# Expert stage of a diffusion step: prompt pieces in groups of three ahead of every third sample chunk

## The chip, the cores and the metric

The kernel runs on one NeuronCore of a Trainium2 chip, in one launch. The metric is the device time of the execution in microseconds (us), taken as the median of several runs. Besides the times there is one profiled execution, whose trace gives every instruction's start and length, what each engine waited for, and the clock that TensorE was granted.

## What is computed

The reference is one layer of a backbone with 1024 latent (sample) tokens and 256 context (prompt) tokens of width 1024, all in float32. After the first sub-layer (convolution and attention) comes the mixture of experts, which takes most of the time:

```python
def expert_choice_ffn(h, w_router, w_gate, w_up, w_down):
    cap = EC_CAPACITY * T // N_EXPERTS          # 128 of 1024 sample tokens, 32 of 256 prompt tokens
    aff = softmax(h @ w_router)
    g, idx = top_k(swapaxes(aff, 1, 2), cap)
    xe = h[idx]
    hid = silu(xe @ w_gate) * (xe @ w_up)       # 1024 -> 2048
    ye = (hid @ w_down) * g                     # 2048 -> 1024
    return zeros.at[idx].add(ye)
```

It is done for the sample tokens and for the prompt tokens with the same weights, for 16 experts. Each expert has 24 MB of weights.

## The kernel before, in words

**Chunks.** The weights of an expert come in 12 chunks of 2 MB (NCH), each with two DMAs from SP's queue into one of six slots: chunks 0 to 7 (NG8 of them) are 256 hidden columns of the gate and of the up matrix, chunks 8 to 11 (ND4) are four blocks of 128 rows of the down matrix. Slot c % 6 takes the next chunk as soon as the sample product of the chunk in it is done.

**Sample product** (`sample(e, c)`, line 1106). For accuracy each weight is split in two parts: ScalarE (ACT) rounds half a chunk at a time into e_hi (`weight_round`, lines 1596 and 1598), of which there are two buffers, and VectorE (DVE) writes the rest over the slot (`weight_rest`, lines 2165 and 2169). TensorE (PE) then runs 24 matmuls 128x512 over the full 128*128 array. The gated result goes ACT (silu, line 1618), DVE (product hid, line 2186), PE (`turn_hid`, two transposes), ACT and DVE (hT_hi and hT_lo, lines 1621 and 2190). Chunk n can be rounded only when sample chunk n-2 has left its e_hi buffer.

**Prompt product** (`prompt(e, c)`, line 1078). It reads the raw weights of the slot, so it must run before `weight_rest` of that chunk. Its 32 rows fill a 128*32 part of the array, four at a time: 128 MATMUL records of 128x128 for two gate and up chunks, 64 of 128x256 for two down chunks. For a gate and up chunk the piece that results goes: `prompt_copy` (ACT, line 1603, bank to pv), `turn_prompt` (PE, line 1146, one transpose), `prompt_gate` (ACT silu, line 1608), `prompt_hid` (DVE product, line 2175). Piece c is in bank 2 + c % 2 throughout, so from chunk 2 on `prompt(e, c)` waits for the product of piece c - 2 (semaphore hp_ok, line 1086).

**Order on PE** (`expert`, line 1151, written out by hand). Ahead of every even sample chunk c a block of two prompt chunks is run, c + 2 and c + 3 (past the end: those of the next expert); then the sample chunk, then `turn_hid(c - 1)`, then `turn_prompt(c + 2)`. After sample chunk 8 come the 16 transposes of the next expert's gathered tokens (`gathered_in`); DVE turns those of the prompt into xpT (`prompt_rows`, line 2145). ACT and DVE have matching orders of their own (lines 1613 and 2178): each of them is a queue in which a wait holds all that follows. Transposes are recorded at line 686, other matmuls at line 683.

Of the kernel before, what the change touches and what calls it, by code (L numbers as in the profile page):

```python
# [25 lines left out]
ALU = mybir.AluOpType  # L26
# [7 lines left out]
P = 128  # L34
# [49 lines left out]
def backbone(nc, A, O):  # L84
    ctx = ExitStack()
    with ctx:
# [110 lines left out]
        sil = at(M7 + 8704, 2, 256)  # L197
        pv = at(M7 + 9216, 2, P)
        psil = at(M7 + 9472, 2, 64)
        xg = at(M7 + 9600, 2, D)  # L200
# [480 lines left out]
        def _(pe):  # L681
# [396 lines left out]
            def prompt(e, c):  # L1078
# [3 lines left out]
                if c < NG8:  # L1082
                    if c == 0:
                        pe.wait_ge(xe_dve, e * KD + KD)
                    if c >= 2:
                        pe.wait_ge(hp_ok, e * NG8 + (c - 1))
                    for k in range(KD):
                        for g in range(4):
                            last = mm(bank[2 + c % 2][32 * g:32 * g + 32, 0:P], xpT[:, k, :],
                                      slot[q][:, 8 * (g // 2) + k, P * (g % 2):P * (g % 2) + P], k == 0, k == KD - 1)  # L1090
                else:
                    f0 = 4 * (c - NG8)
                    pe.wait_ge(hp_ok, e * NG8 + (f0 // 2 + 2))
                    for f in range(f0, f0 + 4):
                        for g in range(4):
                            last = mm(bank[7][32 * g:32 * g + 32, 0:256], hpT[:, f, :],
                                      wide(slot[q])[:, f - f0, 256 * g:256 * g + 256], f == 0, f == KE - 1)
# [44 lines left out]

            def turn_prompt(e, c):

                pe.wait_ge(pv_ok, e * NG8 + (c + 1))
                tr(bank[2 + c % 2][:, 256:256 + P], pv[:, c % 2, :], P).then_inc(pt_ready, 1)

# [3 lines left out]
            def expert(e, last_one):  # L1151

                for c in range(NCH):
                    if e == c == 0:
                        sample(e, c)
                    if c % 2 == 0:
                        for n in (c + 2, c + 3):
                            if n < NCH or not last_one:
                                prompt(*ahead(e, n))
                    if e or c:  # L1160
                        sample(e, c)
                    if 1 <= c <= NG8:
                        turn_hid(e, c - 1)
                    en, cn = ahead(e, c + 2)
                    if cn < NG8 and (en == e or not last_one):
                        turn_prompt(en, cn)
                    if c == NG8 and not last_one:
                        pe.wait_ge(hp_ok, e * NG8 + NG8)
                        gathered_in(e + 1)
# [5 lines left out]
            prompt(0, 1)  # L1175
            turn_prompt(0, 0)
            turn_prompt(0, 1)
            for e in range(NE - 1):
# [5 lines left out]
        def _(act):  # L1184
# [414 lines left out]

            def prompt_copy(e, c):  # L1600

                act.wait_ge(pr_ready, e * NCH + (c + 1))
                A_(pv[:, c % 2, :], bank[2 + c % 2][:, 0:P], ACT.Copy).then_inc(pv_ok, 1)

            def prompt_gate(e, c):

                act.wait_ge(pt_ready, e * NG8 + (c + 1))
                A_(psil[:, c % 2, :], bank[2 + c % 2][:, 256:320], ACT.Silu).then_inc(psil_ok, 1)

# [3 lines left out]
            def expert(e, last_one):  # L1613

                for c in range(NCH):
# [10 lines left out]
                    en, cn = ahead(e, c + 1)  # L1626
                    if cn < NG8 and (en == e or not last_one) and (e, c) != (0, 0):
                        prompt_gate(en, cn)
                    if en == e or not last_one:
                        weight_round(en, cn, 0)  # L1630
                    if c % 2 == 0:
                        for n in (c + 2, c + 3):
                            ep, cp = ahead(e, n)
                            if cp < NG8 and (ep == e or not last_one):
                                prompt_copy(ep, cp)
                    if en == e or not last_one:
# [12 lines left out]
            xe_leave(0, 0, KD)  # L1649
            xe_round(0)  # L1650
            prompt_copy(0, 0)
            prompt_copy(0, 1)
            prompt_gate(0, 0)
            prompt_gate(0, 1)
            for e in range(NE - 1):
# [14 lines left out]
        def _(dve):  # L1670
# [500 lines left out]

            def prompt_hid(e, c):

                dve.wait_ge(psil_ok, e * NG8 + (c + 1))
                V_.tensor_tensor(hpT[:, 2 * c:2 * c + 2, :], bank[2 + c % 2][:, 320:384].rearrange("p (a n) -> p a n", a=2),
                                 psil[:, c % 2, :].rearrange("p (a n) -> p a n", a=2), ALU.mult).then_inc(hp_ok, 1)

            def expert(e, last_one):
# [4 lines left out]
                for c in range(NCH):  # L2183
# [8 lines left out]
                    en, cn = (e, c + 1) if c + 1 < NCH else (e + 1, 0)  # L2192
                    if 0 < c and cn < NG8 and (en == e or not last_one):
                        prompt_hid(en, cn)
                    if c == NG8 + 1 and not last_one:
# [11 lines left out]
                    elif not last_one:  # L2207
                        weight_rest(e + 1, 0)
                if not last_one:
                    prompt_hid(e + 1, 1)  # L2210
                dve.wait_ge(down_ready, e * ND4 + 8)
# [10 lines left out]
            weight_rest(0, 0)  # L2222
            prompt_hid(0, 0)
            prompt_hid(0, 1)
            for e in range(NE - 1):
# [33 lines left out]
```

## Time and profile before

| what | value |
|---|---|
| median of 3 runs | 2732.86 us (2730.2 to 2734.89) |
| the profiled execution | 2732.86 us, of which its span is 2731.1 us |
| PE busy, share of the span | 2606.7 us, 95% |
| DVE, ACT, POOL busy | 65%, 48%, 9% |
| mean granted clock of TensorE | 0.981 of full speed |
| bytes moved | 543.82 MB, mean 199 GB/s; 281 GB/s in the expert stage |

The span runs from the first to the last instruction. A busy share is an average over the whole span. Times of rows count from the span's start. The expert stage begins at about 1171 us, with the first gathered tokens, and ends at about 2690 us. Matmuls overlap one another: a record's length is its latency, and the time that a matmul takes in a stream is the distance between the starts of two of them.

### The profile page before, as it was taken

Reading aid. Unit: us, or ns where it says so; the run is one execution under the profiler, and the core shown is the slowest. Engines: PE = TensorE matmul, PEld = TensorE weight load, DVE = VectorE, ACT = ScalarE, POOL = GpSimd, SP = SyncE. Lnnn points to the kernel's source line nnn. Section 1 sums busy time; section 2 is a strip of 40 time slices with the busy share of each in tenths; the row PEclk is TensorE's granted clock in tenths of the full one; section 3 lists DMA queues with packets and bytes.
Section 4 is the critical chain, followed back from the end, with each engine's and each line's share of the span. In section 5 each row is a group of like instructions: output and inputs, shape, how many; then the busy total and the mean of one; then the engine's idle time right before and its main releaser. Section 6 shows DMA issues by size and latency. Waiting matters only on the chain.

```text
span 2731.1 us, 50488 instructions
## 1 busy us (share of the span) xinstructions
PE 2606.7 (95%) x22107; PEld 2070.5 (76%) x22107; DVE 1776.8 (65%) x2129; ACT 1315.1 (48%) x1911; POOL 239.3 (9%) x194
## 2 busy tenths in 40 slices
PE   5999999999999999779999999999999999999994
PEld 4888866666878887567788778777877877787783
DVE  5699847776343354757667767767767767767664
ACT  5111145555232232456556556555555556556554
POOL 0122012210000000001011001101100110111000
PEclk9999999999999999889999999999999999999997
DMA  8431311001333651668889888879988987988884
GB/s 265 155 93 32 81 48 27 15 24 47 93 93 93 183 172 61 213 206 281 281 279 294 271 279 291 280 265 298 295 259 286 297 269 270 297 273 281 281 268 172
DMA packets 457509, 543.82 MB, mean 199 GB/s; under 512 B 26304, under 2 KB 409387, under 8 KB 457290
## 3 DMA queue, kind: packets, MB, share of 16 engines
q1 hardware_dynamic: 449610, 519.60, 58.3%
q0 software_dynamic: 7680, 20.98, 3.5%
q8 instruction: 176, 2.88, 0.5%
q14 instruction: 43, 0.35, 0.0%
HBM read 513.27 MB, written 27.28 MB: 198 GB/s over the span
## 4 chain that ended last, share of the span: by engine, by line
PE 90%; DVE 3%; ACT 2%; SPq 1%; issue 1%; DMA 1%; POOL 0%; DVEq 0%; POOLq 0%; ACTq 0%
PE bank L683 86%; PE bank L686 4%; SPq L404 1%; DVE arena L1889 1%; ACT arena L1377 1%; DVE arena L1899 0%; DVE arena L2235 0%; DMA arena<-in_w_ada 0%; ACT arena L1381 0%; DMA arena<-in_w_attn_o 0%; DMA arena<-xhat,arena 0%; DVE slot_lo L2165 0%; DVE arena L1896 0%; DMA yacc<-arena 0%; ACT arena L1365 0%
## 5 line engine op out<-in xcount | busy, mean ns | idle before, releaser
L2165 DVE TENSOR_TENSOR slot_lo<-slot,e_hi 128x2048 fp32r<-128x2048 f32 x256 | 579.3, 2289 | 165.2 <-ACT e_hi L1596 163.9
L1596 ACT ACTIVATE e_hi<-slot 128x2048 fp32r<-128x2048 f32 x256 | 481.4, 1917 | 0.0
L683 PE MATMUL bank<-e_hi,xe_hi 128*128 128x512 f32 x1024 | 418.2, 408 | 1.5 <-DVE slot_lo L2165 1.4
L683 PE MATMUL bank<-e_hi,xe_lo 128*128 128x512 f32 x1024 | 404.7, 395 | 0.0
L683 PE MATMUL bank<-slot_lo,xe_hi 128*128 128x512 f32 x1024 | 400.3, 391 | 0.0
L683 PE MATMUL bank<-arena 128*64 128x128 f32 (+9 forms) x2724 | 358.8, 362 | 19.5 <-ACT arena L1377 5.1
L683 PE MATMUL bank<-slot,arena 128*32 128x128 f32 (+1 forms) x10240 | 362.8, 296 | 3.4 <-DVE arena L2149 2.0
L2169 DVE TENSOR_TENSOR slot_lo<-slot,e_hi 128x2048 fp32r<-128x2048 f32 x128 | 288.8, 2288 | 77.9 <-ACT e_hi L1598 77.9
L683 PEld LDWEIGHTS bank<-slot,arena 128*32 128x32 f32 x10240 | 283.9, 110 | 70.6 <-issue 32.2
L683 PEld LDWEIGHTS bank<-arena 128*64 128x64 f32 (+3 forms) x2724 | 245.1, 156 | 104.2 <-issue 43.6
L686 PE MATMUL bank<-arena 128*128 128x128 f32 (+3 forms) x1415 | 204.2, 277 | 54.0 <-DVE arena L1712 12.7
L1598 ACT ACTIVATE e_hi<-slot 128x2048 fp32r<-128x2048 f32 x128 | 239.4, 1912 | 29.5 <-PE bank L683 29.5
L686 PEld LDWEIGHTS bank<-arena 128*128 128x128 f32 (+3 forms) x1415 | 163.4, 143 | 114.0 <-issue 77.1
L683 PEld LDWEIGHTS bank<-e_hi,xe_hi 128*128 128x128 f32 x1024 | 191.9, 187 | 60.6 <-issue 16.1
L683 PEld LDWEIGHTS bank<-slot_lo,xe_hi 128*128 128x128 f32 x1024 | 192.4, 188 | 47.5
L1618 ACT ACTIVATE arena<-bank 128x256 f32<-128x256 f32 x128 | 49.2, 385 | 356.1 <-PE bank L683 356.1
L683 PEld LDWEIGHTS bank<-e_hi,xe_lo 128*128 128x128 f32 x1024 | 192.5, 188 | 37.0
L1803 DVE SCALAR_TENSOR_TENSOR arena<-arena 128x1310 f32<-128x1310 f32 x120 | 213.7, 1781 | 3.9
L683 PE MATMUL bank<-e_hi,hT_hi 128*128 128x512 f32 x512 | 209.4, 409 | 0.0
L683 PE MATMUL bank<-e_hi,hT_lo 128*128 128x512 f32 x512 | 202.3, 395 | 0.0
L683 PE MATMUL bank<-slot_lo,hT_hi 128*128 128x512 f32 x512 | 200.0, 391 | 0.0
L664 POOL DMA_INDIRECT yacc<-arena x16 | 45.7, 2859 | 1311.2 <-DVE arena L2216 1311.2
(244 smaller groups left out, 3622.7 us busy)
## 6 DMA issues: line engine op xcount, KB each, us to landing
slot<-in_w_gate_e SPq DMA_DIRECT2D x128, 1024.0 KB, 5.8
slot<-in_w_up_e SPq DMA_DIRECT2D x128, 1024.0 KB, 9.3
slot<-in_w_down_e SPq DMA_DIRECT2D x128, 1024.0 KB, 6.9
arena<-in_w_in SPq DMA_DIRECT2D x68, 512.0 KB, 5.2
arena<-in_w_ada SPq DMA_DIRECT2D x48, 512.0 KB, 7.4
arena<-in_w_conv_pw SPq DMA_DIRECT2D x24, 256.0 KB, 5.6
arena<-in_w_attn_o SPq DMA_DIRECT2D x24, 256.0 KB, 5.4
yacc<-arena SPq DMA_DIRECT2D x10, 512.0 KB, 2.6
```

The costliest lines, as they stand in the source:

```text
L404: sp.dma_start(ws[s][:, k0:k0 + 4, :], w_ada[:, k0:k0 + 4, ds(n0, 2 * P)]).then_inc(ws_in[s], 16)
L664: nc.gpsimd.indirect_dma_start(out=yacc, out_offset=bass.IndirectOffsetOnAxis(ap=sidx[:, 0:1].bitcast(U32), axis=0), in_=ye, in_offset=Non ...
L683: return nc.tensor.matmul(out, lhsT, rhs, start=start, stop=stop)
L686: return nc.tensor.transpose(out, in_, ident[0:n, 0:n])
L1377: A_(Pctx[g % 2][h][:, 0:n], bank[3 + h][:, 0:n], ACT.Exp, bias=m, accum_out=sums[:, g % 2, h, 1:2]).then_inc(pc_ok, 1)
L1596: A_(halves(e_hi[c % 2])[:, :, rows4, :], halves(slot[q])[:, :, rows4, :], ACT.Copy).then_inc(ehi_ok, 1)
L1598: A_(e_hi[c % 2][:, 8 * h:8 * h + 8, :], slot[q][:, 8 * h:8 * h + 8, :], ACT.Copy).then_inc(ehi_ok, 1)
L1618: A_(sil[:, (c - 1) % 2, :], bank[(c - 1) % 2][:, 0:256], ACT.Silu).then_inc(silu_ok, 1)
L1803: V_.scalar_tensor_tensor(out=conv[:, k, :], in0=glu[:, k, t:t + CONV_W], scalar=dw[:, k, t:t + 1], in1=conv[:, k, :], op0=ALU.mult, op1=A ...
L1889: V_.tensor_reduce(mx[:, g % 2, h, 1:2], bank[3 + h][:, 0:n], AX_X, ALU.max).then_inc(c_max, 1)
L2165: V_.tensor_tensor(halves(slot_lo[q])[:, :, rows4, :], halves(slot[q])[:, :, rows4, :], halves(e_hi[c % 2])[:, :, rows4, :].bitcast(F32), ...
L2169: V_.tensor_tensor(slot_lo[q][:, rows8, :], slot[q][:, rows8, :], e_hi[c % 2][:, rows8, :].bitcast(F32), ALU.subtract).then_inc(elo_ok, 1)
```

## The change

Prompt chunks go in blocks of three (c + 1, c + 2, c + 3) ahead of every sample chunk c with c % 3 = 0, with a special order at the start of expert 0. The pieces of a block lie side by side in bank 2, 128 columns each; the groups of pieces of an expert (TRIO) are chunk 0, chunks 1 to 3, 4 to 6, and chunk 7. One copy moves a group to pv, `turn_prompt` writes its transposes side by side into bank 3, and one gate and one product serve the group. Before the first block's chunk of a group PE waits for the copy of the group before (pv_ok), and `turn_prompt` waits for the product of the group before (hp_ok). The copy stands in ACT's iterations with c % 3 = 0, gate and product in the iterations after them. pv and psil move to another address and are larger.

```diff
--- before.py
+++ after.py
@@ -195,8 +195,18 @@
         hpT = at(M7 + 7680, KE, CAP_P)
         hid = at(M7 + 8192, 2, 256)
         sil = at(M7 + 8704, 2, 256)
-        pv = at(M7 + 9216, 2, P)
-        psil = at(M7 + 9472, 2, 64)
+        pv = at(M7 + 12928, 3 * P)
+        psil = at(M7 + 12928 + 3 * P, 3, 64)
+        TRIO = [(0, 1), (1, 4), (4, 7), (7, 8)]
+
+        def trio_cols(n):
+            c0, c1 = TRIO[n]
+            return slice(P * ((c0 - 1) % 3), P * ((c0 - 1) % 3) + P * (c1 - c0))
+
+        def trio_part(n, half):
+            c0, c1 = TRIO[n]
+            i = (c0 - 1) % 3
+            return bank[3][:, 0:3 * P].rearrange("p (i n) -> p i n", i=3)[:, i:i + c1 - c0, 64 * half:64 * half + 64]
         xg = at(M7 + 9600, 2, D)
         ye = at(M7 + 11648, D)
         yep = at(M7 + 12672, 256)
@@ -1082,15 +1092,16 @@
                 if c < NG8:
                     if c == 0:
                         pe.wait_ge(xe_dve, e * KD + KD)
-                    if c >= 2:
-                        pe.wait_ge(hp_ok, e * NG8 + (c - 1))
+                    if c in (1, 4, 7) and e + c > 1:
+                        pe.wait_ge(pv_ok, e * len(TRIO) + (c + 2) // 3)
+                    c0 = P * ((c - 1) % 3)
                     for k in range(KD):
                         for g in range(4):
-                            last = mm(bank[2 + c % 2][32 * g:32 * g + 32, 0:P], xpT[:, k, :],
+                            last = mm(bank[2][32 * g:32 * g + 32, c0:c0 + P], xpT[:, k, :],
                                       slot[q][:, 8 * (g // 2) + k, P * (g % 2):P * (g % 2) + P], k == 0, k == KD - 1)
                 else:
                     f0 = 4 * (c - NG8)
-                    pe.wait_ge(hp_ok, e * NG8 + (f0 // 2 + 2))
+                    pe.wait_ge(hp_ok, e * len(TRIO) + (2, 2, 3, 4)[c - NG8])
                     for f in range(f0, f0 + 4):
                         for g in range(4):
                             last = mm(bank[7][32 * g:32 * g + 32, 0:256], hpT[:, f, :],
@@ -1140,10 +1151,16 @@
                     last = tr(bank[4][:, P * j:P * j + P], hid[:, c % 2, P * j:P * j + P], P)
                 last.then_inc(ht_ready, 1)
 
-            def turn_prompt(e, c):
-
-                pe.wait_ge(pv_ok, e * NG8 + (c + 1))
-                tr(bank[2 + c % 2][:, 256:256 + P], pv[:, c % 2, :], P).then_inc(pt_ready, 1)
+            def turn_prompt(e, n):
+
+                G = e * len(TRIO) + n
+                pe.wait_ge(pv_ok, G + 1)
+                if G:
+                    pe.wait_ge(hp_ok, G)
+                cols = trio_cols(n)
+                for c in range(cols.start, cols.stop, P):
+                    last = tr(bank[3][:, c:c + P], pv[:, c:c + P], P)
+                last.then_inc(pt_ready, 1)
 
             def ahead(e, c):
                 return (e, c) if c < NCH else (e + 1, c - NCH)
@@ -1153,19 +1170,24 @@
                 for c in range(NCH):
                     if e == c == 0:
                         sample(e, c)
-                    if c % 2 == 0:
-                        for n in (c + 2, c + 3):
+                    if e == c == 0:
+                        turn_prompt(0, 0)
+                        prompt(0, 2)
+                        prompt(0, 3)
+                    elif c % 3 == 0:
+                        for n in range(c + 1, c + 4):
                             if n < NCH or not last_one:
                                 prompt(*ahead(e, n))
                     if e or c:
                         sample(e, c)
                     if 1 <= c <= NG8:
                         turn_hid(e, c - 1)
-                    en, cn = ahead(e, c + 2)
-                    if cn < NG8 and (en == e or not last_one):
-                        turn_prompt(en, cn)
+                    if c % 3 == 0 and c and (c < 9 or not last_one):
+                        turn_prompt(*((e, c // 3 + 1) if c < 9 else (e + 1, 0)))
+                    elif c == 0 and e or e == 0 and c == 1:
+                        turn_prompt(e, 1)
                     if c == NG8 and not last_one:
-                        pe.wait_ge(hp_ok, e * NG8 + NG8)
+                        pe.wait_ge(hp_ok, e * len(TRIO) + len(TRIO))
                         gathered_in(e + 1)
 
             pe.wait_ge(kt_ok, 1)
@@ -1173,8 +1195,6 @@
             gathered_in(0)
             prompt(0, 0)
             prompt(0, 1)
-            turn_prompt(0, 0)
-            turn_prompt(0, 1)
             for e in range(NE - 1):
                 expert(e, False)
             expert(NE - 1, True)
@@ -1597,15 +1617,20 @@
                 else:
                     A_(e_hi[c % 2][:, 8 * h:8 * h + 8, :], slot[q][:, 8 * h:8 * h + 8, :], ACT.Copy).then_inc(ehi_ok, 1)
 
-            def prompt_copy(e, c):
-
-                act.wait_ge(pr_ready, e * NCH + (c + 1))
-                A_(pv[:, c % 2, :], bank[2 + c % 2][:, 0:P], ACT.Copy).then_inc(pv_ok, 1)
-
-            def prompt_gate(e, c):
-
-                act.wait_ge(pt_ready, e * NG8 + (c + 1))
-                A_(psil[:, c % 2, :], bank[2 + c % 2][:, 256:320], ACT.Silu).then_inc(psil_ok, 1)
+            def prompt_copy(e, n):
+
+                act.wait_ge(pr_ready, e * NCH + TRIO[n][1])
+                A_(pv[:, trio_cols(n)], bank[2][:, trio_cols(n)], ACT.Copy).then_inc(pv_ok, 1)
+
+            def prompt_gate(e, n):
+
+                act.wait_ge(pt_ready, e * len(TRIO) + n + 1)
+                A_(psil[:, 0:TRIO[n][1] - TRIO[n][0], :], trio_part(n, 0), ACT.Silu).then_inc(psil_ok, 1)
+
+            def trio_at(e, c):
+                if (e, c) in ((0, 0), (0, 1)):
+                    return (0, 1) if c else None
+                return None if c % 3 else (e, c // 3 + 1) if c < 9 else (e + 1, 0)
 
             def ahead(e, c):
                 return (e, c) if c < NCH else (e + 1, c - NCH)
@@ -1624,15 +1649,16 @@
                     elif c > NG8:
                         act.wait_ge(down_ready, e * ND4 + (c - NG8 + 4))
                     en, cn = ahead(e, c + 1)
-                    if cn < NG8 and (en == e or not last_one) and (e, c) != (0, 0):
-                        prompt_gate(en, cn)
+                    if (e, c) == (0, 1):
+                        prompt_gate(0, 0)
+                    before = trio_at(e, c - 1) if c else None
+                    if before and (before[0] == e or not last_one):
+                        prompt_gate(*before)
                     if en == e or not last_one:
                         weight_round(en, cn, 0)
-                    if c % 2 == 0:
-                        for n in (c + 2, c + 3):
-                            ep, cp = ahead(e, n)
-                            if cp < NG8 and (ep == e or not last_one):
-                                prompt_copy(ep, cp)
+                    now = trio_at(e, c)
+                    if now and (now[0] == e or not last_one):
+                        prompt_copy(*now)
                     if en == e or not last_one:
                         weight_round(en, cn, 1)
                     if not last_one:
@@ -1648,10 +1674,8 @@
             A_(marks[:, 10:11], eps, ACT.Copy).then_inc(down_ready, 4)
             xe_leave(0, 0, KD)
             xe_round(0)
+            act.wait_ge(pr_ready, 2)
             prompt_copy(0, 0)
-            prompt_copy(0, 1)
-            prompt_gate(0, 0)
-            prompt_gate(0, 1)
             for e in range(NE - 1):
                 expert(e, False)
             expert(NE - 1, True)
@@ -2169,11 +2193,17 @@
                         V_.tensor_tensor(slot_lo[q][:, rows8, :], slot[q][:, rows8, :], e_hi[c % 2][:, rows8, :].bitcast(F32),
                                          ALU.subtract).then_inc(elo_ok, 1)
 
-            def prompt_hid(e, c):
-
-                dve.wait_ge(psil_ok, e * NG8 + (c + 1))
-                V_.tensor_tensor(hpT[:, 2 * c:2 * c + 2, :], bank[2 + c % 2][:, 320:384].rearrange("p (a n) -> p a n", a=2),
-                                 psil[:, c % 2, :].rearrange("p (a n) -> p a n", a=2), ALU.mult).then_inc(hp_ok, 1)
+            def prompt_hid(e, n):
+
+                dve.wait_ge(psil_ok, e * len(TRIO) + n + 1)
+                c0, c1 = TRIO[n]
+                V_.tensor_tensor(hpT.rearrange("p (i a) n -> p i (a n)", a=2)[:, c0:c1, :], trio_part(n, 1), psil[:, 0:c1 - c0, :],
+                                 ALU.mult).then_inc(hp_ok, 1)
+
+            def trio_at(e, c):
+                if (e, c) in ((0, 0), (0, 1)):
+                    return (0, 1) if c else None
+                return None if c % 3 else (e, c // 3 + 1) if c < 9 else (e + 1, 0)
 
             def expert(e, last_one):
 
@@ -2190,8 +2220,11 @@
                         V_.tensor_tensor(hT_lo[:, 2 * c - 4:2 * c - 2, :], bank[4][:, 0:256].rearrange("p (a n) -> p a n", a=2),
                                          hT_hi[:, 2 * c - 4:2 * c - 2, :].bitcast(F32), ALU.subtract).then_inc(hlo_ok, 1)
                     en, cn = (e, c + 1) if c + 1 < NCH else (e + 1, 0)
-                    if 0 < c and cn < NG8 and (en == e or not last_one):
-                        prompt_hid(en, cn)
+                    if (e, c) == (0, 1):
+                        prompt_hid(0, 0)
+                    before = trio_at(e, c - 1) if c else None
+                    if before and (before[0] == e or not last_one):
+                        prompt_hid(*before)
                     if c == NG8 + 1 and not last_one:
                         prompt_rows(e + 1)
                     if c == NG8 + 2:
@@ -2206,8 +2239,6 @@
                         weight_rest(e, c + 1)
                     elif not last_one:
                         weight_rest(e + 1, 0)
-                if not last_one:
-                    prompt_hid(e + 1, 1)
                 dve.wait_ge(down_ready, e * ND4 + 8)
                 for h in range(2):
                     cols = slice(512 * h, 512 * h + 512)
@@ -2220,8 +2251,6 @@
             prompt_rows(0)
             xe_rest(0)
             weight_rest(0, 0)
-            prompt_hid(0, 0)
-            prompt_hid(0, 1)
             for e in range(NE - 1):
                 expert(e, False)
             expert(NE - 1, True)
```

## Rows read from the trace of the kernel before

**Rows 1.** The page, busy time of each engine, then the chain that ended last
```profile
PE 2606.7 (95%) x22107; PEld 2070.5 (76%) x22107; DVE 1776.8 (65%) x2129; ACT 1315.1 (48%) x1911; POOL 239.3 (9%) x194
...
PE 90%; DVE 3%; ACT 2%; SPq 1%; issue 1%; DMA 1%; POOL 0%; DVEq 0%; POOLq 0%; ACTq 0%
```
**Rows 2.** Windows: stretch, length, busy us of each engine, clock, DMA, GB/s
```profile
1500.00:1800.00 300.00, 299.88 (x3094) 239.17 (x3096) 209.14 (x203) 176.51 (x209) 25.90 (x12) 1.00 0.85 281
```
**Rows 3.** Waits, 1250 to 2690 us: engine line <- releaser: us, times, longest
```profile
PEld bank L683 <- issue: 52.3, 212, 0.5
```
**Rows 4.** Timeline of PE around a block of two: start, length, line, tiles, shape, count
```profile
1737.16 0.39 PE L683 MATMUL bank<-slot_lo,hT_hi 128*128 128x512 f32 x1
1737.48 3.70 PE L683 MATMUL bank<-slot,arena 128*32 128x128 f32 x128
1741.11 0.51 PE L683 MATMUL bank<-e_hi,hT_hi 128*128 128x512 f32 x1
1741.45 0.40 PE L683 MATMUL bank<-e_hi,hT_lo 128*128 128x512 f32 x1
```
**Rows 5.** Timeline of PE, from within that block
```profile
1738.27 2.68 PE L683 MATMUL bank<-slot,arena 128*32 128x128 f32 x90
```
**Rows 6.** Timeline of PE around one transpose between two sample chunks
```profile
1746.56 0.39 PE L683 MATMUL bank<-slot_lo,hT_hi 128*128 128x512 f32 x1
1746.79 0.27 PE L686 MATMUL bank<-arena 128*128 128x128 f32 x1
...
1747.14 0.40 PE L683 MATMUL bank<-e_hi,hT_lo 128*128 128x512 f32 x1
```
**Rows 7.** Timeline of PE around a block of prompt chunks 4 and 5
```profile
1672.93 0.39 PE L683 MATMUL bank<-slot_lo,xe_hi 128*128 128x512 f32 x1
1673.16 0.49 PE L686 MATMUL bank<-arena 128*128 128x128 f32 x3
...
1677.74 0.39 PE L683 MATMUL bank<-e_hi,xe_lo 128*128 128x512 f32 x1
```
**Rows 8.** Timeline of PE around a block of prompt chunks 6 and 7
```profile
1688.75 0.39 PE L683 MATMUL bank<-slot_lo,xe_hi 128*128 128x512 f32 x1
...
1693.60 0.40 PE L683 MATMUL bank<-e_hi,xe_lo 128*128 128x512 f32 x1
```
**Rows 9.** Timeline of DVE and of PE's weight loads in the block of rows 7
```profile
1672.28 2.28 DVE L2165 TENSOR_TENSOR slot_lo<-slot,e_hi 128x2048 fp32r<-128x2048 f32 x1
...
1675.15 0.21 DVE L2175 TENSOR_TENSOR arena<-bank,arena 128x64 f32<-128x64 f32 x1
...
1675.48 1.61 PEld L683 LDWEIGHTS bank<-slot,arena 128*32 128x32 f32 x60 [0.22 <-issue]
```
**Rows 10.** Timeline of PE, expert 0: first matmuls after a wait, with idle and releaser
```profile
1197.09 0.50 PE L683 MATMUL bank<-e_hi,xe_hi 128*128 128x512 f32 x1 [1.44 <-DVE slot_lo L2165]
...
1202.85 1.95 PE L683 MATMUL bank<-slot,arena 128*32 128x128 f32 x64 [0.49 <-DVE arena L2175]
```
**Rows 11.** Timeline of ACT, expert 0: a copy and the rounding ahead of 1197 us
```profile
1192.63 0.28 ACT L1603 ACTIVATE arena<-bank 128x128 f32<-128x128 f32 x1 [1.47 <-PE bank L683]
1192.81 1.91 ACT L1596 ACTIVATE e_hi<-slot 128x2048 fp32r<-128x2048 f32 x1
```
**Rows 12.** Timeline of PE at the end of a sample chunk, 1704 us
```profile
1704.62 0.39 PE L683 MATMUL bank<-slot_lo,xe_hi 128*128 128x512 f32 x1
```
**Rows 13.** Timeline of ACT, then of DVE, after that chunk
```profile
1705.05 0.38 ACT L1618 ACTIVATE arena<-bank 128x256 f32<-128x256 f32 x1 [1.53 <-PE bank L683]
...
1705.59 0.23 ACT L1608 ACTIVATE arena<-bank 128x64 f32<-128x64 f32 x1
1705.70 3.73 ACT L1596 ACTIVATE e_hi<-slot 128x2048 fp32r<-128x2048 f32 x2
...
1707.72 4.50 DVE L2165 TENSOR_TENSOR slot_lo<-slot,e_hi 128x2048 fp32r<-128x2048 f32 x2 [0.61 <-ACT e_hi L1596]
```
**Rows 14.** The weights' DMAs, 1300 to 2600 us, issue to landing
```profile
DMA to landing us min/median/max: 4.8/7.2/11.8
```

## The prediction

> **What bounds the kernel now.** I read the page first, for one fact: PE is busy for 95% of the span and makes 90% of the chain that ended last [rows 1]. Then the windows, to see where this holds: in 300 us from the middle of the expert stage PE is busy for 299.88, at the full granted clock (1.00, the 2.4 GHz level), while DVE has 209 and ACT 177 of the 300 [rows 2]. So the time changes only by what PE issues and by what it waits for within this stage; work taken from ACT or DVE is worth nothing in itself. A busy PE isn't a PE at its peak, however: a wait shorter than the latency of the matmul before it doesn't show as idle. So the third view is that of the waits. It has one PE row of weight, PE's weight loads that wait for 52.3 us in 212 places, the longest 0.5 us [rows 3]. The fourth is PE's timeline at the borders between kinds of work, read by distances between starts.
>
> **The price of a block.** Two sample matmuls start 0.232 us apart: the 22 steps from 1741.45 to 1746.56 take 5.11 us [rows 4, 6]. Around a block of two prompt chunks, the last sample matmul before it starts at 1737.16, so its place in the stream ends at 1737.39; the second one after it starts at 1741.45, so the stream would have been resumed at 1741.22. The block thus took 3.83 us [rows 4]. Inside it, matmuls come in fours: 90 records take 2.68 us including the last one's latency of about 0.27, which is 22 steps of 0.109 us [rows 5]. 128 records are 32 fours, 3.50 us. The remaining 0.33 us is the price of going over to the small tiles and back: 1737.16 to 1737.48 is 0.32 instead of 0.23, 1741.11 to 1741.45 is 0.34 instead of 0.23, and the rest is at the block's own first and last matmuls [rows 4].
>
> **The change part by part.**
>
> *Fewer blocks.* Before there are 96: [0,1] at the start, six per expert, and one less at the end. After, expert 0 has [0,1], [2,3], [4,5,6], [7,8,9], [10,11, next 0], the experts 1 to 14 have four each and the last has four: 5 + 56 + 4 = 65. All prompt chunks remain. 31 blocks fewer at 0.33 us are **10.2 us**.
>
> *Borders that no block had before*, in the middle of a block: chunk 7 to 8 (gate and up to down, 16 times) and 11 to the next 0 (15 times), 31 in all. Both sides use 128*32 tiles, only the moving width changes from 128 to 256. The bounds are nothing and a whole switch, 0.33 us each. I take nothing: within a block of one kind, going on to the second chunk, in other weights and another bank, leaves 22 even steps of 0.109 [rows 5], and that is the nearest row.
> A rule bears on this. The Trainium skill, "TensorEngine Tiling (Array Packing)", section Key Properties, says that changing the tiling mode, not just the tile, drains TensorE. The trace agrees as far as it goes, with 0.33 us around a block whose tiles are 128*32; by the page the mixed border would cost nothing. If it drained there too, the sum would be 10.2 us worse, which is the first rival.
>
> *The wait in the middle of a block.* For gate and up chunks from 2 on, line 1086 waits for the product of the piece two before. With chunk 5 that product is made only just then: three transposes and the block of 4 and 5 take from 1673.16 (1672.93 + 0.23) to 1677.51 (1677.74 - 0.23), 4.35 us; without 3 transposes of 0.11 (below) and the 3.83 of a free block, 0.19 us is left [rows 7]. DVE's product ends at 1675.36, and PE's weight loads go on at 1675.48 after 0.22 of idle time [rows 9]; DVE was late because the rest of an earlier chunk held it until 1674.56. Chunks 6 and 7 give 4.39 in the same way (1688.98 to 1693.37), so 0.23 us [rows 8]. The trace has 15 blocks of the first kind (experts 1 to 15) and 16 of the second: 15 x 0.19 + 16 x 0.23 = 6.5 us, and the [4,5] of expert 0 idles for 0.49 [rows 10]. After, such a chunk waits only at the head of a group, for the copy of the group before, made at least two sample chunks (over 11 us) earlier; and the product is waited for in `turn_prompt`, a block and a sample chunk later. The down chunks 8 and 9 in the third block need groups 0 and 1, done four sample chunks earlier. So **7.0 us** go and nothing comes in their place.
>
> *Start of expert 0.* Sample chunk 1 waits 1.44 us for the second half of its rest [rows 10], because ACT's rounding of that half stood behind the copies of chunks 2 and 3, which waited for PE until 1192.63 [rows 11]. After, ACT rounds both halves right after its first copy, with no copy between: **1.4 us** go. The two first transposes move from ahead of sample chunk 0 to behind it; ahead of it PE waits for the first rest anyway, so that this costs up to 0.1, taken as 0.
>
> *Transposes.* Their number stays at 8 per expert; one alone costs 0.58 us from 1746.56 to 1747.14, less two steps of 0.232: 0.11 [rows 6]. A group of three is three times that. Nothing gained; the bounds of grouping them are 0 and, if only one per group cost anything, 4 x 16 x 0.11 = 7 us. The triples of rows 7 fit 0.11 each, so 0.
>
> *ACT and DVE.* 4 copies, gates and products per expert instead of 8 each. One copy of 128 columns is 0.28 us [rows 11], of 256 is 0.38 [rows 13]; one of 384 is estimated at 0.48. This is hidden either way, unless the order makes it late. The point to check is the rounding of chunk n, which must fit between the end of sample n - 2 and the start of sample n. Before, there is always one block in that interval. After, for one n in three (2, 5, 8, 11) there is none, and the group's gate and product stand ahead of that very rounding. Count from the start of the last matmul of sample n - 2 [rows 12, 13]: silu at 0.43, gate at 0.97, rounding at 1.08, first rest at 3.10 (1707.72). With five transposes instead of three before the gate I add 0.25: first rest 3.35 to 5.6, second to 7.85. PE starts sample n at 0.23 + 5 x 0.11 + 24 x 0.232 + 2 x 0.11 = 6.6 and needs the second half at 9.4. Both are in time, by 1.0 and 1.5 us. Behind the waiting copy in the iterations with c % 3 = 0 is the second half of chunk c + 1: it now starts some 1.8 us later, but is needed only after half of sample chunk c + 1, over 8 us later. `prompt_rows` of the next expert, wanted one sample chunk earlier than before, has the 3.5 us of chunks 10 and 11 as cover.
>
> *Weights.* The third chunk of a block must be there some 1.8 us sooner than before: its load is issued after sample chunk c - 3, and between come two sample chunks, transposes and two prompt chunks, 11.1 + 0.8 + 3.5 = 15 us. Landing takes 7.2 us in the median and 11.8 at most [rows 14]. Cost 0.
>
> **Sum:** 10.2 + 7.0 + 1.4 = 18.6 us. The profiled execution took 2732.86 us with a span of 2731.1, so 1.8 lie around it; it is also the median of the runs shown. 2732.9 - 18.6 = **2714 us**, 0.7% faster. About 0.2% (5.5 us) can be told from no change.
>
> **Rivals.**
> 1. *The switch is paid in mixed blocks too* (31 borders at 0.33 us). For it: no block before mixes widths. Against: no trace of a cost where the chunk changes. 2714 + 10.2 = 2724 us. 9%.
> 2. *The mid-block wait returns elsewhere*, at the block's head or in `turn_prompt`, because DVE's queue is as late as before (a rest held it until 1674.56 [rows 9]). For it: the same chain copy, transpose, gate, product remains. Against: it has a sample chunk more. 2714 + 7 = 2721 us. 8%.
> 3. *Slower: the interval without a block is too short.* If DVE or ACT enters it one half chunk late (2.25 us, half of the 4.50 in rows 13), the first half is 1.25 us late, 4 times per expert: 64 x 1.25 = 80 us, 2794 us. It decides against the change once the lateness beyond my reckoning passes 1.0 + 18.6/64 = 1.3 us. For it: the margin is the thinnest in the design and DVE has 4.50 us of rests and three short products, some 5.4 in all, for 6.35 of interval. Against: the order of each queue up to there, followed above. 5%.
> Both 1 and 2 together leave 1.4 us, within 0.2%: 4% for no change to tell, late weights included.
>
> **How the numbers follow.** The forecast has 74%, its own range is 2710 to 2718. Rivals 1 and 2 are faster too, so faster has 91%, same 4%, slower 5%. The range goes from 2710 to 2724, which takes in rival 2 and rival 1's middle.
>
> **What would show it.** In the changed trace: 65 blocks, three-chunk blocks of 3 x 1.75 + 0.33 = 5.6 us for three gate and up chunks, no wait inside them; PE's weight loads waiting for far less than 52 us; no idle of 1.44 near 1195 us; expert period shorter by 2 x 0.33 + 0.42 = 1.1 us. Wrong, if [7,8,9] shows a gap at its first 256-wide matmul, if sample chunks 2, 5, 8, 11 start or pause with L2165 or L2169 as releaser, or if a block waits for a slot.

## The result, and the profile after

The changed kernel takes 2738.32 us (median of 12 runs, 2735.12 to 2741.24) against 2732.03 us of the kernel before (12 runs). The ratio is 1.0023 with a 95% interval of 1.0015 to 1.0031: slower by a little, where 0.7% faster was forecast. (One of the kernel before's 12 runs, 2773.62 us, was in a slower state of the chip and is left out of the ratio.) The profiled execution took 2738.47 us with a span of 2736.7 us, 5.6 us more than before. All three savings of the forecast are in the trace, and a pause that it did not know of takes more than they bring.

The page after, busy time, then the chain that ended last by engine, to be held against [rows 1]:

```profile
PE 2595.4 (95%) x22107; PEld 2078.3 (76%) x22107; DVE 1769.5 (65%) x2065; ACT 1302.1 (48%) x1783; POOL 231.0 (8%) x194
```
```profile
PE 90%; DVE 3%; ACT 2%; issue 2%; DMA 1%; SPq 0%; POOL 0%; DVEq 0%; ACTq 0%; POOLq 0%
```

PE is 11 us less busy, although the time went up, and "issue", waiting for nothing that the profile shows, has risen from 1% to 2% of the chain. The windows say where, beside [rows 2]:

```profile
1500.00:1800.00 300.00, 295.65 (x3012) 238.67 (x3014) 207.62 (x191) 174.58 (x183) 24.55 (x12) 1.00 0.85 281
```

PE now idles 4.35 of 300 us in the middle of the expert stage, where it idled 0.12. The waits of 1250 to 2690 us name no other engine for it (before there was one such wait of PE, 0.3 us, and [rows 3]):

```profile
PEld bank L693 <- issue: 49.4, 122, 2.4
...
PE bank L693 <- issue: 19.0, 15, 2.1
```

Two of the 15 in PE's timeline, both in experts' blocks of three gate and up chunks (64 records each):

```profile
1275.65 0.40 PE L693 MATMUL bank<-slot_lo,hT_hi 128*128 128x512 f32 x1
1275.97 5.21 PE L693 MATMUL bank<-slot,arena 128*32 128x128 f32 x180
1283.06 0.63 PE L693 MATMUL bank<-slot,arena 128*32 128x128 f32 x12 [1.87 <-issue]
1283.62 0.50 PE L693 MATMUL bank<-e_hi,xe_hi 128*128 128x512 f32 x1
1283.96 0.40 PE L693 MATMUL bank<-e_hi,xe_lo 128*128 128x512 f32 x1
...
1308.09 1.07 PE L693 MATMUL bank<-slot,arena 128*32 128x128 f32 x30 [2.00 <-issue]
```

The block begins at the usual pace, runs 180 of its 192 records, stops for 2.1 us from start to start, and does the last 12. No instruction there has a semaphore to wait for: the waits on slots and on other engines stand only at a chunk's first matmul, that is after 0, 64 or 128 records. Twelve of the 15 pauses lie inside such a block, three on one of the first sample matmuls behind it.

**The places of the pauses.** Counted over PE's whole instruction stream (weight loads, matmuls and semaphore instructions together, all 45,046 of them in the trace), the 15 pauses of the expert stage come ahead of instruction 16065, 16577, 21953, 22465, 24513, 27841, 28353, 30401, 33729, 34241, 35777, 36289, 39617, 41665 and 42177. Each is 193 past a multiple of 256, without exception (counted from the first instruction that the trace records; why the rest is 193 and not 0, no run shows). The DMA view shows what comes in such units: instructions. From 1280.5 to 1281.7 us:

```profile
q1 hardware_dynamic: 411, 0.41, 102.6%
q8 instruction: 1, 0.02, 5.7%
```

This queue moved 176 packets in the run, 2.88 MB, so 16,384 bytes each, and 45,046 instructions over 176 packets are 256 to a packet. This one started at 1280.54, took 1.09 us and landed at 1281.63; PE went on at 1283.06. In all 15 pauses PE goes on 1.2 to 1.6 us after the packet's landing. PE had run out of instructions.

The Trainium skill, "Runtime: NRT & Kernel Launch", section Instruction fetch mechanics, says that each engine's sequencer fetches its instructions itself in blocks of 16 KiB (256 instructions) through a DMA queue of its own, ahead of need, and calls the cost mostly hidden. The trace agrees with the size, and with a queue whose packets match PE's instructions alone; that the cost is hidden holds for the kernel before and not here, where single pauses reach 2.3 us.

**The clock.** After two of the pauses (2.05 and 2.39 us from start to start) TensorE's granted clock fell to half, 1.2 GHz, for 3.4 us each; after four others of 2.05 to 2.27 us it did not:

```profile
1972.40:1976.00 3.60, 3.60 (x10) 2.79 (x10) 1.44 (x1) 2.13 (x2) 0.00 (x0) 0.53 0.36 139
```
```profile
1972.83 0.63 PE L693 MATMUL bank<-slot_lo,xe_hi 128*128 128x512 f32 x1
1973.26 0.63 PE L693 MATMUL bank<-e_hi,xe_hi 128*128 128x512 f32 x1
```

Sample matmuls start 0.43 us apart there instead of 0.23. For the 8 matmuls of such a stretch that is 1.6 us. In the kernel before the clock did not fall once between 1180 and 2695 us.

**The sum, closed.** From start to start the 15 pauses add up to 23.4 us, 22.1 of them beyond the usual step (the 19.0 us of the view leave out what the last matmul's latency covers). The clock adds 3.2. The forecast of -18.6 us, +22.1, +3.2, and a gain of 3.0 that is told below, make +3.7. Measured from the first prompt matmul to the last sample matmul, the expert stage grew from 1516.1 to 1521.0 us, by 4.9; the other 0.7 us of the span lie outside it. Some 1.2 us are not assigned (4.9 less 3.7).

### The profile page after: what moved, and what is told of

Same layout as the page of the kernel before. It is cut to its first block, busy times and chain, and to the rows that moved or that the text cites. A ratio compares the mean times of both kernels' runs of the same rounds, so it can differ in the third digit from the quotient of the medians.

```text
span 2736.7 us, 50311 instructions
## 1 busy us (share of the span) xinstructions
PE 2595.4 (95%) x22107; PEld 2078.3 (76%) x22107; DVE 1769.5 (65%) x2065; ACT 1302.1 (48%) x1783; POOL 231.0 (8%) x194
## 3 DMA queue, kind: packets, MB, share of 16 engines
q8 instruction: 176, 2.88, 0.4%
## 4 chain that ended last, share of the span: by engine, by line
PE 90%; DVE 3%; ACT 2%; issue 2%; DMA 1%; SPq 0%; POOL 0%; DVEq 0%; ACTq 0%; POOLq 0%
PE bank L693 86%; PE bank L696 5%; DVE arena L1913 1%; ACT arena L1397 1%; DVE arena L1923 0%; DMA arena<-in_w_attn_o 0%; ACT arena L1687 0%; DMA arena<-in_x_sample 0%; ACT arena L1401 0%; DMA arena<-xhat,arena 0%; DVE arena L1736 0%; DMA yacc<-arena 0%; ACT arena L1385 0%; DMA arena<-yacc 0%; DVE w_down L1957 0%
## 5 line engine op out<-in xcount | busy, mean ns | idle before, releaser
L693 PE MATMUL bank<-slot,arena 128*32 128x128 f32 (+1 forms) x10240 | 353.8, 295 | 18.4 <-issue 16.4
```

The costliest lines, as they stand in the source:

```text
L693: return nc.tensor.matmul(out, lhsT, rhs, start=start, stop=stop)
```

## The experiments

The theory: the instruction packets come too late in a block of three gate and up chunks, which has 384 instructions in 5.2 us, where a block of two has 256 and is followed by a sample chunk with 48 in 5.6 us. The rivals: the third slot lands late; ACT and DVE are late in the interval without a block (rival 3 of the prediction).

### e1: half the instructions in the same time

```diff
-                        for g in range(4):
+                        for g in (0, 3):
                             last = mm(bank[2][32 * g:32 * g + 32, c0:c0 + P], xpT[:, k, :],
```


> The changed kernel, but each gate and up prompt chunk runs only column groups 0 and 3 of the four (the other two, half of the prompt's hidden values, are left out). The four groups of a step run side by side, so the PE time of a block should stay at 5.2 + 0.33 us while its instructions fall from 384 to 192. Instruction theory (PE's instruction stream runs dry in blocks of three gate and up chunks, because packets of instructions come late): no idle of PE put down to issue, about 24 us faster than the changed kernel, 2711 to 2716 us. Rival 'late weights' (a slot's DMA lands late for the third chunk) and rival 'late rounding' (ACT and DVE behind in the interval without a block): weights, ACT and DVE are as they were, so the stalls stay, 2733 to 2740 us.

2707.59 us, ratio 0.9924 (0.9907 to 0.9940) to the kernel before, 2729.7 us in that session. No idle of PE put down to issue is left; PE's weight loads wait 26.2 us instead of 49.4. The blocks of three keep their length: from the last sample matmul before to the second after, less two steps, 5.56 us, where the changed kernel without a pause has 5.57. So the four column groups do run side by side, and it is the number of instructions that decides. The time is 3.4 us below the range expected. It is 22.1 us below the kernel before, and without the pauses that is what the change should bring: 18.6 forecast, and the 3.0 told below. Both rivals fall for the pauses, since weights, ACT and DVE were as before.

### e5: three quarters of them

```diff
-                        for g in range(4):
+                        for g in (0, 1, 3):
```


> The changed kernel with column groups 0, 1 and 3 of each gate and up prompt chunk (a quarter of the prompt's hidden values is left out): 288 instructions in a block of three instead of 384, in the same PE time. Instruction theory: 288 is near the 256 of a block of two, which runs without stalls, so at most one or two stalls are left, 2709 to 2716 us. Rivals 'late weights' and 'late rounding': as the changed kernel, about 2736 us.

2707.64 us, ratio 0.9908 (0.9891 to 0.9924), no pause; 24.1 us below the kernel before and 1.4 below the range expected. 288 instructions in 5.2 us are supplied, 384 are not.

### e4: twice the instructions, in the kernel before

```diff
-                            last = mm(bank[2 + c % 2][32 * g:32 * g + 32, 0:P], xpT[:, k, :],
-                                      slot[q][:, 8 * (g // 2) + k, P * (g % 2):P * (g % 2) + P], k == 0, k == KD - 1)
+                            for w in range(2):
+                                last = mm(bank[2 + c % 2][32 * g:32 * g + 32, 64 * w:64 * w + 64], xpT[:, k, :],
+                                          slot[q][:, 8 * (g // 2) + k, P * (g % 2) + 64 * w:P * (g % 2) + 64 * w + 64],
+                                          k == 0 and w == 0, k == KD - 1 and w == 1)
```


> The kernel before, with each gate and up prompt matmul of 128 columns made as two of 64 columns: the same products, twice the instructions of a block (512 instead of 256). Instruction theory: the stalls of the changed kernel come up in the kernel before too: idle of PE put down to issue, more than 19 us of it; block time itself may grow as well if PE cannot take instructions twice as fast, which the distance between the starts inside a block tells apart. Rivals 'late weights' and 'late rounding': no new stalls between the matmuls of a block, only the block's own length changes.

3085.44 us, ratio 1.1292 (1.1271 to 1.1314). A block of two in its timeline:

```profile
1514.46 3.79 PE L683 MATMUL bank<-slot,arena 128*32 128x64 f32 x248
1523.23 0.65 PE L683 MATMUL bank<-slot,arena 128*32 128x64 f32 x8 [4.98 <-issue]
```

248 of 256 records in 3.8 us: PE takes twice as many instructions in the same time without effort, until they run out. PE's idle put down to issue is 174.5 us between 1250 and 2690. The expert stage of this kernel lasts until 3049 us; from 1180 to 3050 it is 226.7 us in 68 pauses, and each pause over 0.7 us lies 193 past a multiple of 256 here too. The rest of the 355.7 us is for the most part the clock, which was at 1.2 GHz for 274 us of the stage and so cost at most 137 (an estimate). So nothing about three chunks, nor about the grouping, is needed for the pause; the rate of instructions over a few us is enough.

### e8: the stream shifted by 32 instructions

```diff
             pe.wait_ge(g1_ok, 7)
+            for _ in range(16):
+                tr(bank[0][:, 0:P], ident, P)
             gathered_in(0)
```


> The changed kernel with 16 further transposes of the identity ahead of the gathered tokens' transposes, in time in which PE waits anyway: 32 instructions (16 matmul records) more ahead of the expert stage, nothing else. Instruction theory: the pauses stay at fixed places of the instruction stream (every one at 193 instructions past a multiple of 256, counted from the start), so each moves 32 instructions earlier in the program: the first two, which left 12 and 30 matmul records of their blocks to do, now leave 28 and 46; the sum of pauses is 20 to 30 us and the time within 5 us of the changed kernel's, 2731 to 2741. If the pauses belong to the block's work (a wait for a slot, ACT or DVE), they stay where they are in the program.

2741.85 us, ratio 1.0035 (1.0023 to 1.0047), a microsecond above what was expected. The two pauses:

```profile
1281.15 1.07 PE L693 MATMUL bank<-slot,arena 128*32 128x128 f32 x28 [0.32 <-issue]
...
1305.16 1.51 PE L693 MATMUL bank<-slot,arena 128*32 128x128 f32 x46 [0.97 <-issue]
```

28 and 46 records left instead of 12 and 30, exactly 32 instructions earlier in the program, and again at 16065 and 16577 of the stream; all 14 pauses (23.8 us from start to start) from expert 1 on are 193 past a multiple of 256. They belong to the stream's packets and not to the work.

### e6: one block of three instead of two

```diff
-        TRIO = [(0, 1), (1, 4), (4, 7), (7, 8)]
+        TRIO = [(0, 1), (1, 4), (4, 6), (6, 8)]
+        BLOCKS = {0: [1, 2, 3], 3: [4, 5], 5: [6, 7], 7: [8, 9], 9: [10, 11, 12]}
```
(12 is chunk 0 of the next expert; columns, waits and the three queues' orders follow the table.)

> Blocks [1,2,3] [4,5] [6,7] [8,9] [10,11,next 0] ahead of sample chunks 0, 3, 5, 7, 9: one block of three gate and up chunks per expert instead of two, and as many blocks as e3. If each such block runs dry by itself, when a packet of instructions happens to be late for it, about half of the changed kernel's stalls stay, some 10 us: 2720 to 2726 us. If it takes two of them close together, the stalls are gone and it equals e3, 2711 to 2716 us. Late rounding: chunks 2 and 11 have an interval without a block, e3 has 8 and 11, so no difference to e3.

2724.07 us, ratio 0.9972 (0.9961 to 0.9984), seven pauses instead of fifteen, 6.6 us of idle instead of 19.0. Each such block runs dry by itself, in those experts in which a packet border falls badly for it.

### e2 and e3: blocks of two, and a mix

e2:

```diff
-        TRIO = [(0, 1), (1, 4), (4, 7), (7, 8)]
+        TRIO = [(0, 1), (1, 3), (3, 5), (5, 7), (7, 8)]
+        BLOCKS = {0: [1, 2], 2: [3, 4], 4: [5, 6], 6: [7, 8], 8: [9, 10], 10: [11, 12]}
```
(The table of groups, columns and waits follow; in e3 the group at chunk 10 moves to 9.)

> Grouped copy, gate and product and both banks as in the changed kernel, but blocks of two: chunks c+1 and c+2 ahead of every even sample chunk c; 96 blocks as before, pieces side by side in one bank. Instruction theory: 256 instructions in a block as in the kernel before, so next to no stalls; what is saved is the wait in the middle of a block (7 us) and the start of expert 0 (1.4 us): 2722 to 2726 us. Rival 'late rounding': nothing to be late, since every interval has a block, the same 2724. Rival 'the product's wait comes back elsewhere': 2731 us.

2721.81 us, ratio 0.9968 (0.9958 to 0.9979): 7.9 us faster than the kernel before, no pause. With the same number of blocks this is the price of the two waits that the grouping removes, forecast at 8.4.

e3, against e2:

```diff
-        BLOCKS = {0: [1, 2], 2: [3, 4], 4: [5, 6], 6: [7, 8], 8: [9, 10], 10: [11, 12]}
+        BLOCKS = {0: [1, 2], 2: [3, 4], 4: [5, 6], 6: [7, 8, 9], 9: [10, 11, 12]}
```

> As e2, but five blocks per expert: [1,2] [3,4] [5,6] ahead of sample chunks 0, 2, 4, then [7,8,9] and [10,11,next 0] ahead of 6 and 9 as in the changed kernel. No block has three gate and up chunks; [7,8,9] and [10,11,0] have 256 instructions. 81 blocks or so instead of 96. Instruction theory: hardly any stall, 5 us less than e2: 2717 to 2721 us. Rival 'late weights': [7,8,9] needs its third slot as early as in the changed kernel, so stalls there, 2725 or more. Rival 'late rounding': chunks 8 and 11 still have the interval without a block, so half of the changed kernel's stalls, about 2731 us.

2713.26 us, ratio 0.9939 (0.9923 to 0.9956), no pause. 16.4 us faster than before, and 4 us below the range expected. Its blocks [7,8,9] and [10,11,0] have 256 instructions, and its chunks 8 and 11 have the interval without a block, so both rivals are refuted here a second time.

### e9: the mix once more

> The kernel of e3 once more, in more rounds, as the version to keep: 0.6% faster than the kernel before (ratio 0.992 to 0.996).

2720.7 us, ratio 0.9961 (0.9947 to 0.9974) to 2731.59 us, just outside what was expected. It remains faster than both kernels, but by 11 us instead of 16, and the intervals only just meet. The profile shows why. Eleven experts have a pause of another kind, 0.6 us from start to start, in the block of chunks 3 and 4. Laid beside e3, the same program, e9 falls back by 0.7 us at each of these places and nowhere else, 7.8 us in all, by which its expert stage is longer (1506.6 against 1498.8 us). One of them, here with POOL's timeline:

```profile
1664.90 3.20 PE L696 MATMUL bank<-slot,arena 128*32 128x128 f32 x105
1668.43 0.90 PE L696 MATMUL bank<-slot,arena 128*32 128x128 f32 x23 [0.33 <-issue]
```
```profile
1667.13 0.88 POOL L669 DMA_INDIRECT arena<-xhat,arena  x1 [0.30 <-issue]
```

These don't sit at a packet's border. They all begin 0.70 to 0.75 us after POOL starts issuing the gather of the prompt rows (0.88 us long). The kernel before has one of them, at 2243.7 us, with the same distance of 0.76, and the changed kernel one in expert 0, at 1191.8 us. In e3 the same gather fell into the same block and PE ran through, so this coincidence is not enough by itself; what more it takes is open.

### e7: more bytes through the DMA engines

```diff
+                n = e * NCH + c - NCH
+                if n >= 0:
+                    s_in, base = spare_in[n % 2]
+                    if n >= 2:
+                        sp.wait_ge(s_in, base + 16 * (n // 2))
+                    sp.dma_start(spare[n % 2], w_g[e, :, 0:2, 256 * (c % 8):256 * (c % 8) + 256]).then_inc(s_in, 16)
```
(The two buffers and the waits for them at the end are left out here.)

> The kernel before, with one further DMA of 256 KB per chunk from expert 1 on (2.25 instead of 2 MB per chunk) into memory that nothing reads. Instruction theory, with packets that are late because they stand in the DMA engines behind weights: packets start later against PE's progress than in the kernel before (1.57 packets' worth of instructions at most there), and some stalls put down to issue appear inside blocks: 5 to 30 us slower. If instructions are late for a reason apart from the weights, the idle put down to issue stays at 0.3 us and the time within 3 us of before, unless a slot is late, which would show at a block's first matmul.

2740.77 us, ratio 1.0035 (1.0024 to 1.0046), so 9 us slower, as the theory in its second part had it. But the reason is not the one expected: the mean rate between 1300 and 2600 us rose from 281 to 312 GB/s and the packets did not get later. Measured in packets' worth of PE's progress, the latest one started at 1.53 (in the kernel before 1.57, in the changed one 1.74), and no pause is at a packet's border. What costs the 9 us is the second kind of pause, in every expert from 1 to 14, 15 in all: at the 0.7 us apiece of e9 they are worth 10.5 (an estimate), and the expert stage grew by 10.6. That packets are late because they queue behind weights is thus not supported; why a packet takes as long as it does was not settled.

## Why the prediction was wrong

Term by term:

- **Fewer blocks, 10.2 us: right.** There are 65 blocks, and one of three gate and up chunks without a pause takes 5.57 us, 48 steps of 0.109 and 0.33.
- **Mixed borders, 0: right.** A block [7,8,9] of the changed kernel:

```profile
1228.53 0.39 PE L693 MATMUL bank<-slot_lo,xe_hi 128*128 128x512 f32 x1
1228.76 0.38 PE L696 MATMUL bank<-arena 128*128 128x128 f32 x2
1229.07 5.41 PE L693 MATMUL bank<-slot,arena 128*32 128x128 f32 x128
...
1234.74 0.39 PE L693 MATMUL bank<-e_hi,xe_lo 128*128 128x512 f32 x1
```

  1234.51 - 1228.76 - 0.22 = 5.53 us. One gate and up chunk is 1.75, two down chunks took 3.45 in the kernel before (4.11 us from 1704.85 to 1708.96, less three transposes and 0.33), the switch is 0.33: together 5.53, and nothing for the border. Rival 1 is out. The rule of the Trainium skill, "TensorEngine Tiling (Array Packing)", section Key Properties, that a change of the tiling mode, not just of the tile, drains the engine, agrees with the row.
- **The wait in the middle, 7.0 us, and the start, 1.4: right in sum.** e2 measured 7.9 for 8.4 (its interval is 5.7 to 11.5). The 1.44 us of sample chunk 1 are gone; sample chunk 0 now shows a wait of 0.8 us for its rest, which before was covered by the transposes. Rival 2 is out.
- **Not forecast, a gain:** the third block of each expert's end, [10,11, next 0], follows the 18 transposes directly. It takes 7.24 us with them (from the row at 1349.51 on, to the second sample matmul after), where 1.905 for transposes alone and 5.53 for the block would be 7.43. Fifteen times 0.2 is 3.0 us. With it, the forecast's terms give 16.4 us for e3 (15 blocks fewer, 5.0; 8.4; 3.0). 16.4 were measured, but that they meet to the tenth is luck: the interval of e3 is some 4.5 us to either side, and e9, the same kernel, gained 10.9.

```profile
1349.51 0.39 PE L693 MATMUL bank<-slot_lo,hT_hi 128*128 128x512 f32 x1
1349.74 1.86 PE L696 MATMUL bank<-arena 128*128 128x128 f32 x18
1351.54 5.41 PE L693 MATMUL bank<-slot,arena 128*32 128x256 f32 x128
...
1357.22 0.40 PE L693 MATMUL bank<-e_hi,hT_lo 128*128 128x512 f32 x1
```

- **Rounding in time by 1.0 us: right.** In the interval of chunk 8 the silu, the group's gate and the two roundings, then DVE:

```profile
1338.23 0.38 ACT L1643 ACTIVATE arena<-bank 128x256 f32<-128x256 f32 x1 [6.90 <-PE bank L693]
...
1338.88 3.74 ACT L1618 ACTIVATE e_hi<-slot 128x2048 fp32r<-128x2048 f32 x2
```
```profile
1340.90 4.49 DVE L2193 TENSOR_TENSOR slot_lo<-slot,e_hi 128x2048 fp32r<-128x2048 f32 x2 [1.37 <-ACT e_hi L1618]
```

  The first rest is done by 1343.15, and PE's two transposes ahead of chunk 8 start at 1343.94, so it is wanted at about 1344.2. Rival 3, the slower case on which the prediction put its 5%, named the wrong mechanism.
- **The step that failed** is the one before all of these: "So the time changes only by what PE issues and by what it waits for within this stage", with the waits looked for among semaphores, slots and other engines alone. The supply of instructions was not on the list, so its term stood at nothing; it measured 22.1 us of pauses and 3.2 of clock. A block was costed as steps of 0.109 us however long it is, and that holds for 256 instructions and not for 384.

**How far a block may go.** The earliest packets of the trace start when PE's own count is 0.59 packets past theirs, and PE runs dry at 1.754, which is 297 instructions later. Two chunks and what follows take over 8 us for these, three chunks in a row 4.1 us. From the point 0.59 to the resumption, the 15 pauses show 4.7 to 6.5 us, 6.2 in the median (3.7 until the packet starts, 1.1 on its way, 1.4 after it). So a block of three falls short by about 2 us, and only where a packet begins near the block's start. The request itself isn't recorded, so this is an estimate. With one fixed 6.2 us, played through the recorded streams without their pauses, it gives pauses at all 15 recorded places of the changed kernel, at all seven of e6, at the 14 of e8 and two more, and at none in the kernel before, e1, e2, e3, e5, e7 and e9. The places come out right, the lengths too long (25.5 us in the changed kernel for 22.1).

**What stays open:** why a packet is so long on its way; whether the second kind of pause, at POOL's gather, has to do with it, and why it came in e9 and not in e3. Nothing lighter in weights' traffic was tried.

## What to carry to other kernels

Where PE runs many small matmuls side by side, count instructions as well as time: here 256 in 3.5 us, then a stretch with few, were supplied, 384 in 5.2 us were not. A pause put down to issue in the middle of a run of equal matmuls, with no wait in the program there, is the sign; here its place modulo the packet size told it from the second kind of pause. Batching small work saves its switches (0.33 us each here) only up to that length, and the best order found has blocks of three where instructions are few and blocks of two where they are many: 2713 to 2721 us against 2730 to 2732.

## What the runs showed of the hardware that was not expected

- PE's instructions come in packets of 256; when they come late PE stands still up to 2.3 us and goes on 1.2 to 1.6 us after the landing.
- Column groups of 128*32 tiles cost nothing in time: two, three or four of them leave the block at 5.56 to 5.57 us.
- A pause of PE of 2 us took the granted clock from 2.4 to 1.2 GHz for 3.4 us in some cases (twice in the changed kernel, four times in e8) and not in others of the same length.
- PE can stop for 0.6 us in a run of small matmuls, 0.7 us after POOL starts an indirect DMA, in one run of a kernel in eleven experts and in another in none.
